# A one-core decoder layer for prompt and sample rows: the head's joint tiles, mixer A in half steps, mixer B in fours of blocks

## The reference

```python
h = rmsnorm(x, g_mix); z = h @ w_in          # 2048 x 5632, columns: qa ka va ga qb kb vb gb
# mixer A: 16 heads, keys t - m*d for (window, d) in (128,1), (512,4), (2048,16), mixed by softmax denominators
s = einsum('nbqgrd,nbkgd->nbgrqk', qb, kk) - slope*dist; p, lse = softmax_lse(s); o = p @ vv
oa = combine_patterns([dilated_prompt(qa, ka, va, d, w // d, slopes) for w, d in DILATIONS])
# mixer B: 16 query heads, 4 key heads, keys t-128..t in blocks of 128 rows, a sink in the denominator
ob = banded_attention(qb, kb, vb, 1, 128, slopes, sinks)
h = x + concat(oa * silu(ga), ob * silu(gb)) @ w_out
h = h + (p @ w_ple) * sigmoid(rmsnorm(h, g_ple) @ w_pg);  y = rmsnorm(h, g_final)
```

## Time and profile before

| | before |
|---|---|
| time, median of three runs | 2342.1 us (2342.1, 2340.39, 2342.34) |
| profiled execution, its time | 2341.7 us |
| its span, first to last instruction | 2339.9 us |
| mean granted TensorE clock | 0.995 |
| busy PE, PEld | 97%, 93% |
| busy DVE, ACT, POOL | 39%, 24%, 33% |
| chain that ended last: PE, DVE, DMA, ACT, POOL | 90%, 4%, 2%, 2%, 1% |

### The profile page before, as it was taken

How to read it: one execution, slowest core, us unless ns; L and a number is a source line. 1 busy time by engine, 2 the same in 40 slices (tenths; PEclk the granted TensorE clock), 3 DMA queues, 4 the chain that set the end, 5 groups by cost and what they waited for, 6 DMA issues and landing times.

```text
span 2339.9 us, 39175 instructions
## 1 busy us (share of the span) xinstructions
PE 2278.0 (97%) x15570; PEld 2179.3 (93%) x15570; DVE 905.0 (39%) x2334; ACT 565.0 (24%) x1562; POOL 771.8 (33%) x783
## 2 busy tenths in 40 slices
PE   4999999999999999999999999999999999999996
PEld 4999999999999999999988999899999999999996
DVE  7123333333324413455555424343233373222235
ACT  5122222222222212323544310210000030000374
POOL 2232222222222133222222233343333344555564
PEclk9999999999999999999999999999999999999998
DMA  5144454444444425455464454454343555444666
GB/s 196 61 125 96 104 117 96 108 114 96 109 111 96 107 71 147 131 147 146 138 160 142 135 174 131 158 139 111 86 102 92 122 164 133 113 115 109 194 202 224
DMA packets 542140, 299.71 MB, mean 128 GB/s; under 512 B 245140, under 2 KB 507300, under 8 KB 540668
## 3 DMA queue, kind: packets, MB, share of 16 engines
q1 hardware_dynamic: 464277, 254.82, 41.1%
q10 hardware_dynamic: 77680, 42.39, 6.3%
HBM read 230.76 MB, written 66.36 MB: 127 GB/s over the span
## 4 chain that ended last, share of the span: by engine, by line
PE 90%; DVE 4%; DMA 2%; ACT 2%; POOL 1%; issue 0%; SPq 0%; DVEq 0%; ACTq 0%; POOLq 0%
PE psum L1081 26%; PE psum L1083 26%; PE psum L1082 26%; PE psum L889 3%; PE psum L911 2%; PE psum L922 2%; PE psum L951 1%; PE psum L979 1%; PE psum L966 1%; DMA h_stage<-h_scratch 1%; DVE x_n L1554 1%; DVE act_lo L1545 1%; PE psum L986 1%; POOL w_lo L845 0%; DMA x_in<-in_x_prompt 0%; DVE act_lo L1912 0%
## 5 line engine op out<-in xcount | busy, mean ns | idle before, releaser
L1081 PE MATMUL psum<-act_hi,w_hi 128*128 128x344 f32 x4032 | 1303.4, 323 | 6.6 <-POOL w_lo L845 5.3
L1083 PE MATMUL psum<-act_hi,w_lo 128*128 128x344 f32 x4032 | 1286.9, 319 | 0.0
L1082 PE MATMUL psum<-act_lo,w_hi 128*128 128x344 f32 x4032 | 1286.1, 319 | 0.0
L1081 PEld LDWEIGHTS psum<-act_hi,w_hi 128*128 128x128 f32 x4032 | 758.2, 188 | 17.9 <-issue 12.4
L1083 PEld LDWEIGHTS psum<-act_hi,w_lo 128*128 128x128 f32 x4032 | 757.5, 188 | 0.0
L1082 PEld LDWEIGHTS psum<-act_lo,w_hi 128*128 128x128 f32 x4032 | 757.2, 188 | 0.2
L843 POOL CAST w_hi<-w_raw 128x512 fp32r<-128x512 f32 (+1 forms) x352 | 222.8, 633 | 1464.1 <-PE psum L1083 1274.9
L845 POOL TENSOR_TENSOR w_lo<-w_raw,w_hi 128x512 fp32r<-128x512 f32 (+1 forms) x390 | 508.7, 1306 | 59.6 <-ACT w_hi L1488 31.3
L1657 DVE COPY prob_t<-psum 128x512 f32<-128x512 f32 (+1 forms) x56 | 35.5, 634 | 391.5 <-PE psum L922 391.5
L1958 DVE TENSOR_TENSOR t_gate<-psum,acc 128x344 f32<-128x344 f32 x48 | 24.7, 515 | 224.9 <-PE psum L1083 224.9
L1889 DVE TENSOR_TENSOR h_row<-psum,h_row 128x344 f32<-128x344 f32 x48 | 22.1, 513 | 212.9 <-PE psum L1083 212.9
(11 more groups left out here) (208 smaller groups left out, 1787.4 us busy)
## 6 DMA issues: line engine op xcount, KB each, us to landing
w_raw<-in_w_in SPq DMA_DIRECT2D x208, 256.0 KB, 3.0
w_raw<-in_w_pg SPq DMA_DIRECT2D x94, 256.0 KB, 2.8
w_raw<-in_w_out SPq DMA_DIRECT2D x64, 256.0 KB, 2.7
z_scratch<-stage ACTq DMA_DIRECT2D x72, 172.0 KB, 1.9
h_scratch<-h_row ACTq DMA_DIRECT2D x16, 516.0 KB, 2.7
x_in<-in_x_prompt SPq DMA_DIRECT2D x8, 1024.0 KB, 5.1
zq<-z_scratch SPq DMA_DIRECT2D x32, 256.0 KB, 3.9
out<-z_sq SPq DMA_DIRECT2D x128, 64.0 KB, 2.8
```

What stands on the lines that cost most here:

```text
L1081: pe.matmul(psum[:, bank, 0:T3], hi_w, hi_a[:, k, rows], start=(k == 0), stop=False, skip_group_check=True)
L1082: pe.matmul(psum[:, bank, 0:T3], hi_w, lo_a[:, k, rows], start=False, stop=False, skip_group_check=True)
L1083: return pe.matmul(psum[:, bank, 0:T3], lo_w, hi_a[:, k, rows], start=False, stop=stop, skip_group_check=True)
```

## The change

**Head.** x_in gets three slots and is normalised in place; the squares go to a tile of their own (x_sq). Constants ident and pick are requested first, g_row when tile 0 has landed. TensorE turns three tiles, then does unit 0 as first_unit: all products with act_hi first, those with act_lo after them. The first six units belong to two weight tiles in turn, (0,0), (1,0), (0,1), (1,1), (0,2), (1,2), in banks 0, 1, 6, 7, 0, 1; for that eight weight groups have places of their own (HEAD_GROUPS), and the act_lo pieces of VectorE and the act_hi copies of ScalarE come in the order of LO_AFTER.

**Mixer A.** A pair has eight half steps. Even ones do values and then scores of two chunks each, odd ones, 27 positions later, only the turns of those two; the next even one is 9 positions behind. Copies go in place into prob; output banks are 6 and 7. Small statistics of several blocks are merged. Requests for V squares and zv move to positions +14 and +36; v_nat, requested before at steps 2 and 4 of the seven (positions +41 and +82), is requested at half steps 2 and 3 (+36 and +63).

**Mixer B.** At s = 0 and 4: values of the four before, then scores of four blocks, both blocks of head 0 ahead of those of head 1. Turns of the four stand alone at s + 3. DVE's bias comes in two portions at s and s+1, its scales at s+1 and s+2; copies go in place.

```diff
-X_LATER = {4: 4, 8: 5, 13: 6, 19: 7, 27: 8}
+X_FIRST = 3
+X_LATER = {12: 3, 17: 4, 26: 5, 39: 6, 44: 7, 48: 8}
+X_BANKS = 24
+LO_AFTER = {1: (0,), 2: (1, 2), 4: (3,), 5: (4, 5), 7: (6,)}
+HEAD_TILES = 2
+HEAD_UNITS = [(i, t) for t in range(3) for i in range(HEAD_TILES)]
+HEAD_BANKS = [0, 1, 6, 7, 0, 1]
+HEAD_GROUPS = 8
+
...
+def unit_of(u):
+
+    return HEAD_UNITS[u] if u < len(HEAD_UNITS) else divmod(u, 3)
+
+
+def last_unit(tile):
+
+    return 2 * HEAD_TILES + tile if tile < HEAD_TILES else 3 * tile + 2
+
+
+def unit_bank(u):
+
+    return HEAD_BANKS[u] if u < len(HEAD_UNITS) else u % 2
...
-SCORE_AT = [0, 2, 3, 4, 5, 6, 8]
-TURN_AT = [7, 4, 5, 6, 8, 9, 10]
-TURN_ORDER = [1, 2, 3, 0, 4, 5, 6]
...
-A_STEPS = 13
...
+A_HALVES = 8
+A_STEPS = 12
+SCORE_AT = [0, 2, 2, 4, 4, 6, 6]
+STEP_FIRST = [0, 1, 1, 3, 3, 5, 5]
+TURN_AT = [9, 3, 3, 5, 5, 7, 7]
+TURN_ORDER = [1, 2, 3, 4, 5, 6, 0]
+FAR_SCALE_AT = 7
+SCORE_SLOT = [0, 0, 1, 0, 1, 0, 1]
+TURN_SLOT = [1, 0, 1, 0, 1, 0, 1]
...
-TURN_B, VALUES_B = 2, 4
-B_BANKS = (4, 7)
+BQ = 4
+TURN_B, VALUES_B = 3, 4
+B_BANKS = (2, 3, 4, 7)
...
+def ring_slot(g):
+
+    return g if g < HEAD_GROUPS else (g - HEAD_GROUPS) % WRING
+
+
+def ring_before(g):
+
+    return None if g < HEAD_GROUPS else g - HEAD_GROUPS if g < HEAD_GROUPS + WRING else g - WRING
...
-        put(16 * (3 * tile + 2) + 4 * (part + 1), "weights", g)
+    for g in range(HEAD_GROUPS + 2, WG * (NZ - 2) + 7):
+        tile, part = divmod(ring_before(g - 2), WG)
+        put(16 * last_unit(tile) + 4 * (part + 1), "weights", g)
...
-        for s in range(NCH if n + 1 < PAIRS else A_STEPS):
-            put(176 + 144 * n + (144 * s // NCH if n + 1 < PAIRS else 14 * s), "a", n, s)
+        for s in range(A_HALVES if n + 1 < PAIRS else A_STEPS):
+            put(176 + 144 * n + (36 * (s // 2) + 27 * (s % 2) if n + 1 < PAIRS else 32 * (s // 2) + 24 * (s % 2)), "a", n, s)
+        put(176 + 144 * n + 14, "a_high", n)
+        put(176 + 144 * n + 36, "a_low", n)
...
 
             for i, (r0, n) in enumerate(ROW_TILES):
-                if i >= 2:
-                    sp.wait_ge(sem("x_normed"), i - 1)
-                sp.dma_start(x_in[0:n, i % 2, :], x_p[r0:r0 + n, :] if i < 8 else x_s).then_inc(sem(f"x_loaded{i % 2}"), 16)
+                if i >= 3:
+                    sp.wait_ge(sem("x_turned"), 4 * (i - 2))
+                sp.dma_start(x_in[0:n, i % 3, :], x_p[r0:r0 + n, :] if i < 8 else x_s).then_inc(sem(f"x_loaded{i % 3}"), 16)
                 if i == 0:
                     sp.dma_start(ident[:], a["c_ident"]).then_inc(sem("consts"), 16)
+                    sp.dma_start(pick[:], a["c_pick"]).then_inc(sem("consts"), 16)
                     sp.wait_ge(sem("x_loaded0"), 16)
                     sp.dma_start(g_row[:], bcast_rows(a["g_mix"][0:1, :], P)).then_inc(sem("consts"), 16)
-                elif i == 1:
-                    sp.dma_start(pick[:], a["c_pick"]).then_inc(sem("consts"), 16)
...
-                for g in {1: (0, 1), 2: (2,), 3: (3,), 5: (4,)}.get(i, ()):
+                for g in {2: (0, 1), 3: (2, 3), 4: (4, 5), 5: (6, 7)}.get(i, ()):
                     weights(g)
...
                     elif s == 2:
-                        load_zv(n, 0)
                         load_v_nat(n, 1)
                     elif s == 3:
-                        store_squares(n, V_LOW)
-                    elif s == 4:
                         load_v_nat(n, 0)
...
+                elif e[0] == "a_high":
+                    store_squares(e[1], V_HIGH)
+                    load_zv(e[1], 0)
+                elif e[0] == "a_low":
+                    store_squares(e[1], V_LOW)
...
+            def first_unit():
+
+                rows = slice(0, T3)
+                pe.wait_ge(sem("x_hi"), 4 * 3)
+                for k in range(KT):
+                    if k in X_LATER:
+                        x_turn(X_LATER[k])
+                    group_wait("in", 0, k)
+                    hi_w, lo_w = split_place(GROUP["in", 0, k - k % WG], WG)
+                    pe.matmul(psum[:, 0, 0:T3], hi_w[:, k % WG, :], act_hi[:, k, rows], start=(k == 0), stop=False, skip_group_check=True)
+                    pe.matmul(psum[:, 0, 0:T3], lo_w[:, k % WG, :], act_hi[:, k, rows], start=False, stop=False, skip_group_check=True)
+                pe.wait_ge(sem("x_lo"), 4 * 3)
+                for k in range(KT):
+                    hi_w = split_place(GROUP["in", 0, k - k % WG], WG)[0]
+                    mm = pe.matmul(psum[:, 0, 0:T3], hi_w[:, k % WG, :], act_lo[:, k, rows], start=False, stop=(k == KT - 1), skip_group_check=True)
...
                 for n, s in a_walked(n_, s_):
-                    if s in SCORE_AT:
-                        a_scores(n, SCORE_AT.index(s))
+                    for c in TURN_ORDER:
+                        if TURN_AT[c] == s - 1:
+                            a_values(n, c)
+                for n, c in a_chunks(n_, s_):
+                    a_scores(n, c)
                 for n, s in a_walked(n_, s_):
-                    if s - 1 in TURN_AT:
-                        a_values(n, TURN_AT.index(s - 1))
-                for n, s in a_walked(n_, s_):
-                    if s in TURN_AT:
-                        a_turns(n, TURN_AT.index(s))
+                    for c in TURN_ORDER:
+                        if TURN_AT[c] == s:
+                            a_turns(n, c)
```

The heart of mixer B in the diff, TensorE's scores and VectorE's two portions:

```diff
+                    for two in range(0, BQ, 2):
+                        for h in range(2):
+                            half = slice(HD * h, HD * h + HD)
+                            for x, b in enumerate((s_ + two, s_ + two + 1)):
+                                k0, nk = max(b - 1, 0) * BLK, BLK * min(b + 1, 2)
+                                mm = pe.matmul(psum[:, B_BANKS[two + h], 256 * x:256 * x + nk], zq[half, b * BLK:(b + 1) * BLK], zkb[half, k0:k0 + nk],
+                                               start=True, stop=True)
+                            mm.then_inc(sem("b_scored"), 1)
...
-                        both = mx[:, (s - 1) % 4:(s - 1) % 4 + 2]
+                    at = s % BQ
+                    if s < QB and at in (1, 2):
+                        b0 = s - 1 if at == 1 else s
+                        dve.wait_ge(sem("b_exped"), (QB * n + b0) // 2 + 1)
...
+                    if s < QB and at < 2:
+                        b0 = s + at
                         if s == 0:
                             dve.wait_ge(sem("biasb_loaded"), 32 * (n + 1))
-                        if n or s >= 4:
-                            dve.wait_ge(sem("b_turned"), QB * n + s - 2)
+                        if at == 0:
+                            if n or s:
+                                dve.wait_ge(sem("b_summed"), QB * n + s)
```

More of the change, by code:

```diff
@@ L415, in a_walked, with a_chunks @@
         def a_walked(n, s):
-            if n and s + NCH < A_STEPS:
-                yield n - 1, s + NCH
+            if n and s + A_HALVES < A_STEPS:
+                yield n - 1, s + A_HALVES
             yield n, s
+        def a_chunks(n_, s_):
+            chunks = [(n, c) for n, s in a_walked(n_, s_) for c in range(NCH) if SCORE_AT[c] == s]
+            return sorted(chunks, key=lambda nc: scored_before(*nc))
         def stored(u):
@@ L570, in a_step @@
                         load_zq("a", n + 1, 0)
-                    for half, at_s in ((1, 9), (0, 12)):
+                    for half, at_s in ((0, 9), (1, 11)):
                         if s == at_s:
@@ L608, in b_step @@
                         load_bias_b(n + 1)
-                    for half, at_s in ((0, 7), (1, 11)):
+                    for half, at_s in ((0, 6), (1, 10)):
                         if s == at_s:
@@ L886, in a_scores @@
                         half = slice(HD * h, HD * h + HD)
-                        if i == 0 and first:
-                            pe.wait_ge(sem("a_biased"), 2 * (first - 1) + h + 1)
-                        mm = pe.matmul(psum[:, 2 + h, col:col + w], queries(half), keys(half), start=True, stop=True)
+                        if i == 0 and h == 0 and first:
+                            pe.wait_ge(sem("a_biased"), 2 * first)
+                        mm = pe.matmul(psum[:, bank + h, col:col + w], queries(half), keys(half), start=True, stop=True)
                         if i == len(pieces) - 1:
@@ L970, in b_step @@
                 for n, s in walked(n_, s_, QB):
                     first = s - TURN_B
-                    if 0 <= first < QB and s % 2 == 0:
-                        if n or first:
-                            pe.wait_ge(sem("b_copied"), QB // 2 * n + first // 2)
-                        for b in (first, first + 1):
+                    if 0 <= first < QB and first % BQ == 0:
+                        for b in range(first, first + BQ):
                             for h in range(2):
@@ L1101, in _ @@
                         group_wait("in", tile, k)
-                    if k == 0 and u >= 2:
-                        pe.wait_ge(sem("bank_free"), u - 1)
```

(27 more changed lines are left out.)

330 lines of the change are left out of this document (162 added, 168 removed).

## The result

The changed kernel takes 2366.86 us (median of four runs, 2362.93 to 2367.51), the kernel before 2342.22 in the same comparison: a ratio of 1.0098, 95% interval 1.0086 to 1.011, 24.6 us. The forecast was 2326, its range ended at 2341.

A forecast was written before the change was run, and what follows sets the result against it. The prediction took TensorE's own work as the bound from 65 us on, with waits for normalised rows in the head. Head -10, mixer A -10 and mixer B +5 gave -15 from 2342.1: 2327, stated as 2326, own range 2314 to 2337, with rivals 2308 to 2341.

The forecast's parts named there:

- Head, forecast -10: Head: units 0 to 2 done in TensorE's gaps, so unit 6 starts near 87.7 instead of 97.53; 9.8 us gained, taken as 10.
- VectorE's new idle time: Head: about 1 us waiting for x tile 1 and about 1.5 us at tile 6 for ScalarE's square.
- Mixer A, forecast -10: Mixer A: 12.6 us gained from fewer array shape changes, less 2.5 us of waits for v_nat.
- The array changes: Mixer A: nine fewer changes of the array's shape per pair of heads at 0.175 us each, 12.6 us for eight pairs.
- 0 to 1.6 us late: I take 0.3 for each pair: Mixer A: lateness of v_nat's low half at a pair's first values, 2.5 us in all.
- 5.7 us of k-steps and 1.5 us of turns: Mixer A: TensorE work expected to cover the load of v_nat's low half, which lands 2.7 to 4.6 us after its request.
- the prediction's own durations: Mixer A, v_nat request: GpSimd's group split 0.63 + 1.31 us, 1 to 2 more if VectorE delays it, load 2.7 to 4.6.
- Mixer B, forecast +5: Mixer B: 8.4 us gained on visits, 3.5 lost to the scores' order and 10 lost to waits; 5 us slower.
- -8.4 + 3.5: Mixer B visits: 8.4 us saved by fewer array changes, 3.5 lost with head 0's scores ahead of head 1's (range 0 to +27).
- the chain worked: Mixer B: VectorE's and ScalarE's steps between scores and turns; first eight fours in time, last eight 14.5 us late against 4.3.
- Rival (2): Mixer B: waits are double, late fours 3 to 4 us later still; +15 us, 2341; chance 0.12.
- rival (4): Mixer B: scores lose their side-by-side run altogether, up to 27 us instead of 3.5; 2350, slower; chance 0.09.

The follow-up runs named there:

- the run of the head alone: The kernel before with only the head part of the change, mixers A and B as before: 2339.14 us, ratio 0.9988.
- the run with the alternating heads: The changed kernel with mixer B's scores alternating between the two heads again, two blocks a bank: 2364.27 us, ratio 1.0091.
- the last two kernels: Changed kernel, v_nat's low half and bias_b requested earlier, both bias/exponential portions in one step, scores alternating, sample's steps later: 2324.73 us; with squares ahead 2324.71.
- mixer A alone: The kernel before with only mixer A's half steps from the change, head and mixer B as before: 2353.01 us, ratio 1.0048.
- the earlier bias: The changed kernel with the next pair's bias_b requested at step 6 of mixer B instead of step 7: 2361.29 us, ratio 1.0071.
- the one-step softmax: The changed kernel with both portions of a four's bias, shift and exponentials in step s of mixer B: 2355.98 us, ratio 1.005.
- three fixes: The changed kernel with v_nat's low half requested at +50, bias_b at step 6, and both portions' bias and exponentials in one step: 2335.87 us, ratio 0.996.
- mixer B alone: The kernel before with only mixer B's fours from the change, head and mixer A as before: 2363.79 us, ratio 1.0088.
- squares ahead: First of the last two kernels, plus ScalarE squaring the next x tile ahead of the act_hi copies from tile 3 on: 2324.71 us, ratio 0.9911.
- the run with B as before: The kernel before with the change's head and mixer A, v_nat's low half requested at +50, mixer B as before: 2328.32 us, ratio 0.9924.

## Why the prediction was wrong

**Head, forecast -10, measured -4.8 (-6.2 in the run of the head alone).** Order and work were as described: units 0, 1 and 2 in the gaps, TensorE waiting 21.5 us for rows. Two terms were too small. VectorE's new idle time was put at 2.5 us; but from its first small instruction to the end of the last x_n it took 54.1 us instead of 49.7, 4.4 more. The rows show 4.1 us of idle time in four waits for ScalarE (before there was one, of 0.75 us); the other 1.1 us are its own instructions, small ones above all, that took longer. The waits:

```profile
15.06 0.15 DVE L1627 TENSOR_SCALAR small<-small 128x1 f32<-128x1 f32 x1 [0.87 <-ACT x_sq L1342]
...
31.31 0.15 DVE L1627 TENSOR_SCALAR small<-small 128x1 f32<-128x1 f32 x1 [1.20 <-ACT x_sq L1342]
...
48.38 2.48 DVE L1621 TENSOR_TENSOR act_lo<-psum,act_hi 128x512 fp32r<-128x512 f32 x4 [1.14 <-ACT act_hi L1339]
51.73 0.16 DVE L1627 TENSOR_SCALAR small<-small 128x1 f32<-128x1 f32 x1 [0.87 <-ACT x_sq L1342]
```

And behind TensorE's last wait for rows, at 65.46, the main products stood at nearly twice their spacing from 68.1 to 72.7 us (16 in 4.58 us instead of 2.51): 2.1 us more. In the run with the alternating heads, whose head is the same program, this didn't happen, and unit 6 started at 90.23 instead of 92.71. Units 3 to 5 took 25.0 us instead of 22.6.

**Mixer A, forecast -10, measured +7.0.** The array changes were sized well: without waits A is 11.2 us shorter, forecast were 12.6, and copies and scales are hidden as said. The step that failed is "0 to 1.6 us late: I take 0.3 for each pair". It was 1.8 on average, 14.3 us instead of 2.5. The cover was counted as "5.7 us of k-steps and 1.5 us of turns", but the 5.7 already hold the turns (9 k-steps are 4.2); the rows show 5.9 in all, against 3.4 until the request and 4.5 until the values. With 5.7 the prediction's own durations (1.94, then 1 to 2, then 2.7 to 4.6 with 3.5 in the middle) would have given 0.7 to 1.7 us late in the middle and 2.8 at the far end. It also let one weight load stand ahead of the request; the queue shows two or three and a store.

**Mixer B, forecast +5, measured +21.9.** Visits: -8.4 + 3.5 was forecast, and -5.4 measured (3.92 and 1.76 us for a four against 6.02 for two twos, sixteen times), though by other parts: the scores' order cost 1.6. Waits: 22.0 us against 4.3, so +17.7 instead of +10; the chain worked had the right place (the late fours, the sample behind the second portion) but let only one product with a silu stand in it, and held the first eight fours free, where a late bias table made one of 3.5 us. The rest of the 21.9, 9.6 us, was in no term: it is the clock, which stood at its lower level for 30.7 us of B's stretch, 22.9 of them with TensorE busy; before it never did there.

**What no step of the prediction had: the clock behind a wait.** It priced a wait at its own length. The stages around one of A's waits, and around B's wait of 5.28 us at 1129 (the last three columns: granted clock, DMA share, GB/s):

```profile
426.00:438.00 12.00, 12.00 (x82) 11.85 (x80) 2.66 (x7) 1.61 (x4) 7.54 (x8) 1.00 0.39 120
438.00:447.00 9.00, 6.84 (x51) 5.04 (x51) 2.26 (x11) 0.59 (x3) 0.00 (x0) 0.81 0.20 56
447.00:456.00 9.00, 9.00 (x60) 9.00 (x59) 3.95 (x17) 3.40 (x13) 0.00 (x0) 1.00 0.32 64
```

```profile
1123.00:1136.00 13.00, 7.72 (x37) 7.40 (x37) 6.62 (x31) 4.52 (x14) 3.75 (x4) 0.74 0.42 127
```

The clock, at 2.4 GHz in the first stretch, stood at 1.2 for part of the middle one and came back; below this is called a fall. A visit with such a fall cost 7.45 us where its neighbour cost 5.57 with a wait only 0.26 shorter. In A the eight waits cost 14.3 us and what hung on them 3.9, most of it the two falls; in B the falls cost about 10 beside 17.7 of waits; in the head 2.1. The Trainium skill, TensorE: Matmul & The Clock Gate, Part 1, says that the throttled state is the default and activity releases it. These rows agree with it in kind, and a price for waits should have had it. With most of the waits the falls went too: none in A once v_nat came early, none in B in the last two kernels, where 6.7 and 8.3 us of waits are left.

So of the 40 us between forecast and result, some 21 are waits that were sized too small (A 11.8, B 7.7, the head's VectorE 1.9), 16 the clock (A 3.9, B 9.6, the head 2.1), and the other 4 us or so the visits (1.4 in A), 1.7 us behind unit 131, and what is left of the head. Rival (2), doubled waits in B, was the nearest in mechanism, with 0.12, but its 2341 had neither A's waits nor the clock; rival (4), 2350, ended on the right side for a wrong reason.

## What to carry to other kernels

When a change thins out the places at which an engine is fed, look on every queue for what stands ahead of each request there: a DMA that was requested 20 k-steps early and now 9 is priced by what blocks the queue, not by its landing time, and all its cover has to be counted once. Where two steps of work are moved into one program order, put the pieces that don't depend on the slow engine ahead of those that do. And price a wait of a saturated TensorE at more than its length: here 32.0 us of new waits in A and B brought 13.5 us more with them, nearly all of it slow products. Cutting such waits was worth more here (18 us in A for one moved DMA) than the visits that the change saved (11).

## What the runs showed of the hardware

The clock's fall behind short waits. In the five runs whose values products waited for v_nat behind weight loads and store (the changed kernel, mixer A alone, the earlier bias, the one-step softmax, the alternating heads), 40 such waits stand between main products at full clock. None of the 23 from 0.67 to 1.91 us was followed by a fall; 12 of the 17 from 1.92 to 2.53 us were, each making the visit 1.7 us longer than its wait did. Waits of 2.34 and 2.37 us passed without one, and one of 1.92 had it, so length alone doesn't decide. At other places it says less still: waits of 2.81 (three fixes), 2.95 (mixer B alone) and 3.20 us (squares ahead) in B passed without a fall, and one of 1.53 us for s_prod had one in mixer A alone and in the run with B as before.

Products on the two halves of the array's rows, into different banks, stay side by side when each half gets two in a row: eight products (16 records) take 2.03 us against 1.93 strictly alternating, and the second half's first starts ahead of the first half's second, against the order of the program (16 visits of 16).
